# Filler products on TensorE and an earlier place for u and the lag tables in the S5 mixer of a bidirectional SSD/S5 kernel

## The reference, cut to what matters

```python
ug = uf.reshape(bsz, seq, 64, 16)                      # 64 groups of 16 channels
bu_re, bu_im = einsum(ug, b_re), einsum(ug, b_im)      # 64 complex states a group
for d in range(2):                                     # both directions
    drive = q * bu                                     # complex
    st = associative_scan(lambda_bar, drive, reverse=(d == 1))
    y_ssm += einsum(st_re, c_re[d]) - einsum(st_im, c_im[d])
y = y_ssm.reshape(bsz, seq, D_MODEL) + d_skip * uf
h = gelu(y) @ w_glu + b_glu
out = h[..., :D_MODEL] * sigmoid(h[..., D_MODEL:])
```

## Time and profile before

| | us |
|---|---|
| median of three runs | 1591.23 |
| lowest, highest | 1587.77, 1592.2 |
| the profiled execution | 1590.69 |
| its span | 1589.0 |
| mean granted TensorE clock, share of full | 0.973 |
| TensorE busy with products / with weight loads | 1517.5 / 1234.7 |
| VectorE / ScalarE / GpSimd busy | 1176.2 / 725.7 / 245.3 |

### The profile page before, as it was taken

One profiled execution on the slowest core, in us unless ns is written; L12 is line 12 of the kernel. 1 busy time (PEld: TensorE's weight loads), 2 busy tenths in 40 slices (PEclk: granted clock), 3 DMA queues, 4 the chain that ended last, 5 costly groups with the idle time before them and its releaser, 6 DMA issues.

```text
span 1589.0 us, 20267 instructions
## 1 busy us (share of the span) xinstructions
PE 1517.5 (96%) x7383; PEld 1234.7 (78%) x7383; DVE 1176.2 (74%) x1362; ACT 725.7 (46%) x1104; POOL 245.3 (15%) x244
## 2 busy tenths in 40 slices
PE   7998999999989999999989989989999999999998
PEld 5866777677667788888876769988888888888886
DVE  6787668778777989988898968965676666743354
ACT  5664545454643655134446341433355555532244
POOL 0345020030127400030075100000100000001001
PEclk9999999999999999999999986979999999999999
DMA  4623244143225333633436497932323333323222
GB/s 122 201 61 113 67 127 139 47 152 108 80 67 106 114 124 132 211 128 125 152 119 207 172 309 232 278 84 93 105 81 102 96 92 105 106 86 99 87 93 87
DMA packets 192234, 199.01 MB, mean 125 GB/s; under 512 B 47886, under 2 KB 178526, under 8 KB 188062
## 3 DMA queue, kind: packets, MB, share of 16 engines
q1 hardware_dynamic: 184510, 192.76, 38.4%
q10 hardware_dynamic: 7648, 5.25, 1.1%
HBM read 169.47 MB, written 28.51 MB: 125 GB/s over the span
## 4 chain that ended last, share of the span: by engine, by line
PE 70%; DVE 15%; issue 5%; DMA 5%; ACT 3%; SPq 1%; POOL 0%; DVEq 0%; ACTq 0%; POOLq 0%
PE ring L2125 21%; PE ring L2126 20%; PE ring L2135 20%; DVE w_lo L1485 2%; PE ring L2392 2%; PE pe_s L2412 2%; DVE cc L1611 2%; DMA w_raw<-in_ssd_w_in 1%; DMA w_raw<-in_ssd_w_out 1%; PE pe_s L2402 1%; ACT w_hi L1047 1%; DVE zs L1796 1%; PE ring L2276 1%; DVE cc L2003 1%; DVE ytmp L1787 1%
## 5 line engine op out<-in xcount | busy, mean ns | idle before, releaser
L2125 PE MATMUL ring<-uh,w_hi 128*128 128x512 f32 (+1 forms) x1160 | 457.8, 395 | 9.8 <-ACT w_hi L1047 4.2
L2126 PE MATMUL ring<-ul,w_hi 128*128 128x512 f32 (+1 forms) x1160 | 452.8, 390 | 0.0
L1047 ACT ACTIVATE w_hi<-w_raw 128x1024 fp32r<-128x1024 f32 (+1 forms) x233 | 239.5, 1028 | 433.0 <-PE ring L2126 335.6
L1485 DVE TENSOR_TENSOR w_lo<-w_raw,w_hi 128x1024 fp32r<-128x1024 f32 (+1 forms) x233 | 288.4, 1239 | 159.2 <-PE ring L2135 125.3
L2135 PE MATMUL ring<-uh,w_lo 128*128 128x512 f32 (+1 forms) x1160 | 289.8, 392 | 7.3 <-DVE w_lo L1485 7.3
L2125 PEld LDWEIGHTS ring<-uh,w_hi 128*128 128x128 f32 (+1 forms) x1160 | 218.2, 188 | 62.0 <-issue 10.7
L2135 PEld LDWEIGHTS ring<-uh,w_lo 128*128 128x128 f32 (+1 forms) x1160 | 218.9, 189 | 54.7 <-DVE w_lo L1485 8.6
L2126 PEld LDWEIGHTS ring<-ul,w_hi 128*128 128x128 f32 (+1 forms) x1160 | 218.1, 188 | 46.8 <-issue 1.6
L2125 PE MATMUL ring<-gh,w_hi 128*128 128x512 f32 x480 | 188.9, 393 | 5.3 <-ACT w_hi L1047 4.0
L2126 PE MATMUL ring<-gl,w_hi 128*128 128x512 f32 x480 | 187.9, 392 | 0.0
L2003 DVE SCALAR_TENSOR_TENSOR cc<-cin,par,cc 128x512 f32<-128x512 f32 x176 | 129.5, 796 | 1.0 <-ACT cc L1408 1.0
(11 more groups left out here) (342 smaller groups left out, 2043.5 us busy)
## 6 DMA issues: line engine op xcount, KB each, us to landing
w_raw<-in_ffn_w_up SPq DMA_DIRECT2D x88, 512.0 KB, 3.5
w_raw<-in_ffn_w_down SPq DMA_DIRECT2D x40, 512.0 KB, 3.4
w_raw<-in_ssd_w_in SPq DMA_DIRECT2D x32, 512.0 KB, 4.1
s_tables<-tab SPq DMA_DIRECT2D x16, 1024.0 KB, 4.7
slot<-s_tables SPq DMA_DIRECT2D x16, 1024.0 KB, 7.8
fwd<-log_decays SPq DMA_DIRECT2D x16, 512.0 KB, 5.3
w_raw<-in_ssd_w_out SPq DMA_DIRECT2D x16, 512.0 KB, 3.5
w_raw<-in_ple_w_gate SPq DMA_DIRECT2D x16, 512.0 KB, 3.5
```

What stands on the lines that cost most here:

```text
L1047: act.activation(w_hi[u % 2][:, 0:n], w_raw[:, u % 2, 0:n], ACT.Copy).then_inc(hi_done, 1)
L1485: dve.tensor_tensor(w_lo[u % 2][:, 0:n], w_raw[:, u % 2, 0:n], w_hi[u % 2][:, 0:n].bitcast(F32), ALU.subtract).then_inc(lo_done, 1)
L2125: pe.matmul(o, wh[:, k, c], rh[:, k0 + k, :], start=first and k == 0, stop=False)
L2126: mm_ = pe.matmul(o, wh[:, k, c], rl[:, k0 + k, :], start=False, stop=False)
```

## The change

On TensorE a helper `keep_clock(n, out)` multiplies two constant tiles, `ones` and `eye` (128 by 128 each), n times into a PSUM bank that nothing reads. It is called after each four transposes of block 1 (2 products each), ahead of `drive(0)` (8), between `within5` and `outputs5` of blocks 0, 6 and 7 (14, 8 and 20, each behind a wait for ScalarE's copies of the transposed tables), and at the program's end between the first and the second sum of squares (8, behind a wait for the last tile's evacuation, which stood further down before). The transposes of block 2 move behind `drive(1)`.

```diff
+                    def keep_clock(n, out):
+                        for _ in range(n):
+                            pe.matmul(out, ones[:], eye[:], start=True, stop=True)
...
                             mm_.then_inc(vt_full, 1)
+                            keep_clock(held, bank(0)[:, 0:P])
...
+                    HELD = {0: 14, NB - 2: 8, NB - 1: 20}
...
-                    v_transposes(1)
-                    v_transposes(2)
+                    v_transposes(1, held=2)
+                    keep_clock(8, bank(0)[:, 0:P])
                     drive(0)
...
                         if b == 0:
+                            v_transposes(2)
                             kernels(2)
                         within5(b)
                         if 0 < b < NB - 2:
...
+                        else:
+                            pe.wait_ge(vt_evac, 4 * min(b + 3, NB))
+                            keep_clock(HELD[b], pe_e[:, 0, 0:P])
                         outputs5(b)
...
                 mm_.then_inc(sq_used, 1)
+                if n == 0:
+                    pe.wait_ge(evac, T["final"])
+                    keep_clock(8, bank(T["final"])[:, 0:P])
             pe.wait_ge(hn_done, KD)
-            pe.wait_ge(evac, T["final"])
```

```diff
                 rotation_load(0)
-                slot_load(2, 0)
-                slot_load(2, 1)
-                rotation_load(1)
                 u_save(0)
                 u_save(1)
                 u_lift(0)
                 u_lift(1)
+                slot_load(2, 0)
+                rotation_load(1)
+                slot_load(2, 1)
...
                 u_save(2)
+                toeplitz_load(0)
                 slot_load(3, 0)
-                toeplitz_load(0)
...
+                    if b + 2 < NB:
+                        toeplitz_load(b + 2)
                     sp.wait_ge(y5_evac, b + 1)
...
-                    if b + 2 < NB:
-                        toeplitz_load(b + 2)
                     sp.wait_ge(y5_saved[b % 2], 16 * LC * (b // 2 + 1))
...
-                    v_out(2)
                     decay_row(1)
                     bq_mask(2)
+                    v_out(2)
```

More of the change, by code:

```diff
@@ L2333, in _, with v_transposes @@
                 if layer == 1:
+                    def keep_clock(n, out):
+                        for _ in range(n):
+                            pe.matmul(out, ones[:], eye[:], start=True, stop=True)
                     def slot_ready(b, kind):
                         pe.wait_ge(slot_in[b % 4][kind], 16 * (b // 4) + 16)
-                    def v_transposes(b, n0=0, n1=4):
+                    def v_transposes(b, n0=0, n1=4, held=0):
                         slot_ready(b, 0)
```

## The result

The forecast was 1575 us. The change made the kernel slower, by 0.55%, and the interval of the ratio lies above 1.

What follows compares the result with a forecast made beforehand. The S5 decides, with TensorE at half clock slower than VectorE's 12.55 us a block in blocks 1 to 3. Terms -5.0 - 8.1 + 0.5 + 1.5 + 1.0 - 3.4 - 2.1 = -15.6 from 1590.69 gave 1575 us, range 1567 to 1587.

Steps and rivals of the forecast that it cites:

- Head, -5.0: Start of the S5: u lands earlier, the drive starts at 940.7 at full clock, VectorE at 944.4; -5.0 us.
- Block 0, +0.5 with bounds 0 and +3: Block 0: lag-0 store behind 2.5 MB of tables makes Toeplitz tables late, TensorE waits about 3.4 us, mostly absorbed; +0.5 us.
- The loop, +1.5 with bounds 0 and +4.3: Loop over blocks: tables ahead of y stores, SyncE's round drifts some 5 us, one clock fall likely; +1.5 us.
- The last two blocks, +1.0 with bounds 0 and +6: Blocks 6 and 7: fillers fit in waits for states, but delay the outputs if block 7's tables are late; +1.0 us.
- Outputs -3.4 and GLU -2.1: After block 7: last outputs at full clock, 7.09 to 3.68 us; GLU's first unit 7.53 to 5.44 us.
- The end of the program, 0: Last sums: eight fillers fill a 1.85 us idle wait; 0, bounds -1.5 and +0.3.
- Pace, -8.1: Blocks 0 to 7: with TensorE at full clock VectorE sets 12.55 us a block; -8.1 us over seven blocks.
- the pace's own sign of being wrong: Blocks of the S5: the pace is wrong if VectorE waits for a drive anywhere from block 2 on.
- the one in which SyncE and the queues take over: Rival, S5 loop: SyncE's round sets the pace in four blocks, late tables drop the clock; 1582 us, chance 0.19.
- The slower rival: Rival, S5: clock at half up to block 3 and fillers on the path; +13.5, 1604 us, chance 0.06.
- Its sign: Block 0, for the slower rival: Toeplitz tables come after 957 and the clock stays at 0.50 through the 14 fillers.
- the one against the loop's term: Loop: its term is wrong if `tz` or the load of y holds no one, or holds TensorE over 2 us a block.

Runs made afterwards that it cites:

- e7: The changed kernel with all of SyncE's list as before, so TensorE's part of the change alone; 1582.3 us, 0.9963 of before.
- e6: e5 with 0, 0 and 8 fillers instead of 14, 8 and 20 in blocks 0, 6 and 7, and four ahead of `within5(7)`; 1582.9 us.
- e9: The changed kernel with the load of y of blocks 0 to 4, and SyncE's waits for it, moved behind the next block's u and tables; 1581.8 us.
- e10: e5 with the Toeplitz tables of block 2 issued ahead of the loop; 1583.9 us.
- e13: The changed kernel with the edits of e9 and e4 together: late load of y, lag-0 store ahead of block 2's tables; 1576.3 us.
- e4: The changed kernel with the lag-0 store ahead of block 2's two tables and block 1's rotations; 1591.6 us.
- e1: The changed kernel with the loop's order taken back, y stores ahead of the Toeplitz tables again; 1584.7 us.
- e2: The kernel before with the loop's new order alone, Toeplitz tables ahead of the y stores, no fillers; 1595.2 us.
- e14: e13 with 12 fillers in place of 20 ahead of block 7's outputs and 4 ahead of `within5(7)`; 1577.8 us.
- e8: The kernel before with SyncE's new order at the head of the S5 alone; 1592.5 us, 1.0049 of before.
- e12: e5 without any filler products; 1585.8 us.
- e5: The changed kernel with the edits of e1 and e4 together: loop's order taken back, lag-0 store ahead of block 2's tables; 1578.6 us.
- e3: The changed kernel with none of its filler products, all places of transfers and transposes kept; 1600.7 us.

## Why the prediction was wrong, step by step

**Head, -5.0: right.** VectorE's first multiply comes 19.9 us after the mark for 24.9, the drive takes 7.33 us for 64 at full clock. The fillers kept it there despite 1.12 us of waiting, and there was luck in that: of the eleven profiles with these same fillers ahead of the drive, eight have it at full clock (behind up to 2.02 us of waiting, e7) and three near half for most of its length (e6, e9 and e10, behind 1.11 to 1.38).

**Block 0, +0.5 with bounds 0 and +3: mis-sized.** The step let the lag-0 store land at 946 to 947, by the bytes ahead of it and 413 GB/s. It took 10.03 us and landed at 949.27. In e13, ahead of the tables, the same 64 KB took 3.6 us. Tables asked for at 949.29 came at 958.98, the idle wait was 8.64 us for a forecast 3.4, the clock fell, and VectorE lost 3.21 and 2.34 us behind it: block 2 started 5.3 us late for the forecast 0.5. e4 prices this term at 6.2 us.

**The loop, +1.5 with bounds 0 and +4.3: this is the step that failed.** The prediction put it so: SyncE's round "grows little" where the queues are the limit, "against VectorE's 12.55 it drifts, from block 1 to 4, by some 5 us, and eats what was gained". It named the exposed landing and then priced it as a drift from a reserve. In fact the rounds became 15.7, 17.3, 17.6 and 16.9 us (lifts of u at 971.15, 986.86, 1004.20, 1021.83 and the next round's tables at 1038.69), some 3 to 5 us above VectorE's pace in each block. A round above the pace is no single drift; its excess is paid again for every block until the loads end. The four rounds exceed VectorE's pace by 17.3 us in sum, and VectorE's starts from block 2 to 7 by 14.7, where the step had put 1.5 and at most 4.3. I also took a DMA share of 1.05 as the limit on the round, which e13 refutes with 1.05 and a round of 11.8. By medians the swap cost 13.0 us on top of the rest of the change (e1), some 6.2 in the kernel before (e2), and moving only the load of y and its wait gave 16.0 back (e9).

Part of it was a chain I had not looked for. The rotations are issued by ScalarE, in order behind its work on TensorE's late results, so a late table also delayed `erot`, and VectorE waited 9.5 us in three places. Before the second and the third of these issues (1010.84 and 1029.67) ScalarE had itself waited 11.99 and 10.18 us for TensorE's transposes. The first (990.94) had no such wait ahead of it; there the landing was long, up to 10.3 us, where in e13 all took 4.2 to 5.5. In e2, with far less waiting on TensorE, it was 3.9 us, in e1 and e13 none.

**The last two blocks, +1.0 with bounds 0 and +6: inside the bounds, at the bad end.** The 20 fillers took 7.02 us instead of 4.7, for the clock had fallen to 0.50 at 1060, behind only 0.78 us of idling (1059.14), and the outputs began at 1068.72, 6.3 us after VectorE's states (1062.45). In e13 and e14, with the blocks in time, the end is 17.6 and 15.5 us for a forecast of 16.3.

**Outputs -3.4 and GLU -2.1: right in after.** 3.68 us for the last outputs, 5.56 us for the first GLU unit (1072.21 to 1077.77). Where the blocks are in time the fillers do not secure it: in e13 and e9 the outputs wait 1.50 us behind them and take 5.96 and 5.68. **The end of the program, 0: right.** From the last sums to the end of the span 10.3 us for 10.65.

**Pace, -8.1: right where the other two causes are gone.** e13 has 87.8 us from block 0 to 7 where the step said 87.85. In after the pace's own sign of being wrong came (VectorE waits 2.34 us for block 2's drive), as a result of block 0's late tables.

**Of the rivals**, the one in which SyncE and the queues take over had the mechanism, the round of SyncE as the pace and a wait in block 0. It was priced at 1582, with two falls of the clock instead of the excess of the round times the blocks it covers. The rows shown already gave the better sum: Toeplitz issue 5.82, y stores 3.72 and a landing of up to 9.14 us, one behind another, are up to 18.7 us a round against VectorE's 12.55, where before the first lay beside the last. The slower rival had another cause, fillers at half clock on the path; in after that is only the 2.3 us at block 7 and some of block 0. Its sign came by half: the tables came after 957 (958.98), but the clock was back at 1.00 before the 14 fillers ended. So it is luck that its 1604 is the price nearest to 1597.8. The stated range of 1567 to 1587 is also wider than its own terms, whose bounds add up to 1570.6 and 1585.4; the result lies outside of both. Of the signs that the prediction named, the drive near 941 at full clock came, and so did the one against the loop's term, tables that hold TensorE over 2 us a block (5.16, 2.67).

What stays open: why e6 with fewer fillers was slower, why a table issued earlier in e10 only moved the wait, and why the clock falls behind one idle wait and not behind another of the same length.

## What to carry to other kernels

On an engine that issues transfers in order, look at what its own waits stand beside: here a landing of 6 to 9 us cost little with 6 us of issue between the stores and the wait, and set the pace with none. Compare the length of the whole round with the pace of the engine it feeds, for a round above the pace is paid every block. And a small store on which others wait did better ahead of the large loads than behind them (e4).

## What the runs showed of the hardware

A store of 64 KB took 3.6 us in front of the tables (e13) and 10.03 us behind 2.5 MB of them (after). A DMA share of 1.05 over ten us (995 to 1005) stood beside TensorE and VectorE without a wait (e13), while in the slower kernel the share in the same stretch was 0.72.

The length of an idle wait did not tell by itself whether the granted clock fell. In after it was 0.50 behind waits of 8.64, 5.16 and 2.67 us, but also from 1060 on behind 0.78, and it stayed at 1.00 in the drive at 939.69 behind 1.12 with fillers ahead. The same drive with the same fillers ran at full clock behind 2.02 us in e7 and took 11.72 us behind 1.11 in e10; without fillers the clock fell behind 1.78. After 8.19 us of idling it rose again amid 16 transposes (e8).

By medians, products of constants were worth 7.3 us in a kernel with 7.2 us of waits for tables (e12 against e5); with 17.5 us of such waits no worth is shown (e3 against after, 2.9 us with overlapping intervals).
